# Low parts of 22 weight chunks in two attentions: GpSimd subtracts instead of VectorE

## The reference, cut to what matters

```python
qz = h @ w_in                                   # 1024 x 4096: q of 24 heads, z
q = rms_norm(q, q_norm_g) * (HEAD_DIM ** -0.5)
o, lse = dilated_group_attn(q[:, :, hs], kb, vb, slopes[hs], window, d)   # three groups
alpha = jax.nn.softmax(jnp.stack(lses), axis=0)
y = o.reshape(bsz, s, B_WIDTH) * jax.nn.silu(z)
```

```python
y_a = chunked_attention(q.reshape(shp), k.reshape(shp), v.reshape(shp), rel_table) @ w_attn_out
y_b = conv_module(c_in, conv_glu_bias, conv_dw_w, conv_dw_b, conv_ln_g, conv_ln_b, conv_w_out)
gates = jax.nn.sigmoid(g + gate_bias)
```

## Time and profile before

| what | us |
|---|---|
| median of 3 runs | 1925.88 (1925.7 to 1926.75) |
| profiled execution, span | 1924.0 |
| PE busy | 1830.6 (95%) |
| DVE busy | 1047.5 (54%) |
| ACT busy | 736.8 (38%) |
| POOL busy | 53.2 (3%) |
| low parts on DVE (L1827) | 149, 337.2 busy, mean 2263 ns |

### The profile page before, as it was taken

The page is one execution under the profiler, slowest core; times in us unless marked ns, Lnnn a source line. Parts: engine busy times, 40 slices in busy tenths (PEclk is TensorE's granted clock), DMA queues, the critical chain, the costliest instruction groups (busy, mean ns, idle before and its releaser), DMA issues.

```text
span 1924.0 us, 22231 instructions
## 1 busy us (share of the span) xinstructions
PE 1830.6 (95%) x8618; PEld 1492.9 (78%) x8618; DVE 1047.5 (54%) x1498; ACT 736.8 (38%) x1008; POOL 53.2 (3%) x103
## 2 busy tenths in 40 slices
PE   4999999989999999999999999998999999999998
PEld 3788888856877777778888887986666788888887
DVE  6336666458566666754444314699775463333213
ACT  4445554224355656432323214223462342323212
POOL 1000001000000000100000000000000000000000
PEclk8999999989999999999999999999999999999999
DMA  8346565422322221233342323232223223342321
GB/s 329 134 131 188 176 176 174 150 77 67 86 66 66 66 61 50 70 104 90 88 125 82 119 89 88 88 110 70 63 66 110 88 69 106 87 119 78 121 88 66
DMA packets 246679, 201.10 MB, mean 105 GB/s; under 512 B 6386, under 2 KB 225860, under 8 KB 245572
## 3 DMA queue, kind: packets, MB, share of 16 engines
q1 hardware_dynamic: 238048, 166.25, 29.3%
q0 software_dynamic: 8064, 33.56, 5.0%
q10 hardware_dynamic: 484, 0.16, 0.0%
HBM read 197.83 MB, written 2.11 MB: 104 GB/s over the span
## 4 chain that ended last, share of the span: by engine, by line
PE 77%; DVE 13%; ACT 5%; issue 3%; DMA 1%; DVEq 0%; SPq 0%; POOL 0%; ACTq 0%; POOLq 0%
PE acc L699 13%; PE acc L701 13%; PE acc L700 13%; PE sc L1064 6%; DVE s_s_row L2163 4%; PE acc L1064 3%; DVE s_w_low L1827 2%; PE tr L1064 2%; ACT s_w_high L1323 2%; PE ob L1064 2%; PE misc L1064 2%; DMA s_ada_w<-in_a_ada_w 1%; PE sc L699 1%; PE sc L701 1%; PE sc L700 1%
## 5 line engine op out<-in xcount | busy, mean ns | idle before, releaser
L1827 DVE TENSOR_TENSOR s_w_low<-s_raw,s_w_high 128x2048 fp32r<-128x2048 f32 (+1 forms) x149 | 337.2, 2263 | 356.4 <-ACT s_w_high L1323 356.4
L1323 ACT ACTIVATE s_w_high<-s_raw 128x2048 fp32r<-128x2048 f32 x151 | 284.6, 1885 | 205.0 <-PE acc L1064 174.6
L699 PE MATMUL acc<-s_h_high,s_w_high 128*128 128x512 f32 x880 | 345.1, 392 | 1.6 <-DVE s_sg L2399 1.6
L701 PE MATMUL acc<-s_h_high,s_w_low 128*128 128x512 f32 x880 | 342.5, 389 | 0.0
L700 PE MATMUL acc<-s_h_low,s_w_high 128*128 128x512 f32 x880 | 342.5, 389 | 0.0
L699 PEld LDWEIGHTS acc<-s_h_high,s_w_high 128*128 128x128 f32 x880 | 165.3, 188 | 37.2 <-issue 4.1
L701 PEld LDWEIGHTS acc<-s_h_high,s_w_low 128*128 128x128 f32 x880 | 165.2, 188 | 34.6
L700 PEld LDWEIGHTS acc<-s_h_low,s_w_high 128*128 128x128 f32 x880 | 165.3, 188 | 33.7 <-issue 0.2
L1699 ACT ACTIVATE s_hid_high<-s_hd 128x512 fp32r<-128x512 f32 x44 | 27.8, 632 | 219.3 <-DVE s_hd L2408 119.0
L890 PE MATMUL acc<-s_h_high,s_w_high 128*128 128x512 f32 x256 | 107.3, 419 | 2.2 <-DVE s_w_low L1827 1.4
L699 PE MATMUL acc<-s_b_high,s_w_high 128*128 128x512 f32 x224 | 91.7, 410 | 11.3 <-DVE s_b_low L1876 7.3
(11 more groups left out here) (446 smaller groups left out, 3353.7 us busy)
## 6 DMA issues: line engine op xcount, KB each, us to landing
s_raw<-in_a_w_in SPq DMA_DIRECT2D x48, 512.0 KB, 5.0
s_raw<-in_ffn_w_gate SPq DMA_DIRECT2D x44, 512.0 KB, 4.0
s_raw<-in_ffn_w_up SPq DMA_DIRECT2D x44, 512.0 KB, 5.2
s_raw<-in_ffn_w_down SPq DMA_DIRECT2D x40, 512.0 KB, 4.2
s_raw<-in_w_in SPq DMA_DIRECT2D x36, 512.0 KB, 4.4
s_raw<-in_b_w_in SPq DMA_DIRECT2D x32, 512.0 KB, 4.8
s_ada_w<-in_b_ada_w POOLq DMA_DIRECT2D x24, 512.0 KB, 4.9
s_ada_w<-in_a_ada_w POOLq DMA_DIRECT2D x8, 1024.0 KB, 12.6
```

What stands on the lines that cost most here:

```text
L699: pe.matmul(bank[b][:, :], w_high[:, o:o + P], hi, start=(k == 0), stop=False, skip_group_check=grouped)
L701: mm = pe.matmul(bank[b][:, :], w_low[:, o:o + P], hi, start=False, stop=(k == nk - 1), skip_group_check=grouped)
L1323: act.activation(w_high[:, part], raw[:, part], ACT.Copy).then_inc(w_high_ready, 1)
L1827: dve.tensor_tensor(w_low[:, w], raw[:, w], w_high[:, w].bitcast(F32), ALU.subtract).then_inc(w_ready, 1)
```

## The change

GpSimd gets a helper `low_part(c)`, which waits for the high part of chunk c, subtracts, and counts `w_ready` up. It does so for chunks 1 to 15 of "qz", for the two of "bo" as before, and for chunks 1 to 7 of "gates"; `tile_sum` moves between the third and the fourth of those. VectorE loses the same 15 subtractions in the loop over (s, n) and seven of the eight in the loop over rows; the one at n = 29, for the first chunk of the next phase, stays with it. All other orders stay.

```diff
--- before.py
+++ after.py
@@ -668,10 +668,16 @@
                                    pattern=[[-1, P]], channel_multiplier=1).then_inc(dist_ready, 1)
 
 
+            def low_part(c):
+
+                w = slice(c % 2 * SLOT, (c % 2 + 1) * SLOT)
+                pool.wait_ge(w_high_ready, c + 1)
+                pool.tensor_tensor(w_low[:, w], raw[:, w], w_high[:, w].bitcast(F32), ALU.subtract).then_inc(w_ready, 1)
+
+            for j in range(1, 16):
+                low_part(C0["qz"] + j)
             for s in range(2):
-                pool.wait_ge(w_high_ready, C0["bo"] + s + 1)
-                w = slice(s * SLOT, (s + 1) * SLOT)
-                pool.tensor_tensor(w_low[:, w], raw[:, w], w_high[:, w].bitcast(F32), ALU.subtract).then_inc(w_ready, 1)
+                low_part(C0["bo"] + s)
 
             def tile_sum():
 
@@ -682,7 +688,11 @@
                 pool.wait_ge(cy_added, 2)
                 pool.tensor_tensor(ln[0][:, :], ln[0][:, :], ln[1][:, :], ALU.add).then_inc(cy_added, 1)
 
-            tile_sum()
+            for g in range(1, 8):
+                if g == 4:
+                    tile_sum()
+                low_part(C0["gates"] + g)
+
         @block.tensor
         def _(pe):
             def product(b, tq, s, where, t, high, low, k0, nk, ready=None, base=0, between=None, bank=acc):
@@ -2235,7 +2245,6 @@
                 dve.reciprocal(tiny[:, Q_R + 12 * (s % 2):Q_R + 12 * (s % 2) + 12], tiny[:, Q_RT:Q_RT + 12])\
                    .then_inc(qr_ready, 1)
 
-            low = None
             a = NQ - 1
             for s in range(NQ):
                 for n in range(4):
@@ -2243,9 +2252,6 @@
                     before = (s - 1, n - 1) if n > 0 else (s - 2, 3)
                     if before[0] >= 0:
                         scale(*before)
-                    if low is not None:
-                        next_low(*low)
-                        low = None
                     if n == 3:
                         query_means(s)
                     if s > 1 and n == 1:
@@ -2260,8 +2266,6 @@
                         query_rstd(s)
                     if s > 1 and n == 2:
                         y_rest(s - 2)
-                    if t is not None and t % 2 == 0 and t < 4 * NQ - 2:
-                        low = q0 + t // 4, t // 2 % 2
             scale(a - 1, 3)
             tops(a, 0)
             near_row(a, 1)
@@ -2564,7 +2568,7 @@
                 e0 = EARLY[1] + 6 * PER_CHUNK + PER_ROW * n
                 for e in range(e0, min(e0 + PER_ROW, len(taps))):
                     tap(e)
-                if n % 4 == 1:
+                if n == H2 * TT - 3:
                     next_low(q0 + n // 8, n // 4 % 2)
                 conv_norm(n - LN_AT)
             scale2(H2 * TT - 1)
```

## The result

The changed kernel takes 1945.62 us in the median of 4 runs (1944.16 to 1946.35), the kernel before beside it 1926.32 (1925.7 to 1927.85): a ratio of 1.0097, 95% interval 1.0084 to 1.011, slower. Forecast were 1942 and a range of 1929 to 1953.

The account below looks back on a forecast made before the run. TensorE was taken as the bound, except VectorE in the second attention while it has convolution taps. First attention 5.1, port 8.2 and clock 3.4 sum to +16.7 on 1924.0, plus 1.9 to the median: 1942, range 1929 to 1953.

Parts of the forecast that it names:

- Start of the first attention: First attention's first chunks: low parts come late with little or no slack, costing 2.3 + 1.3 + 1.7 = 5.3 us.
- Steady slots: Five first-attention slots: 2.34 us gained and 2.6 lost in each, taken as +0.1 to +0.3 a slot, +0.5 in all.
- Last slot: First attention, 738 to 768 us: its single chunk is 0.3 us late, but its rows come sooner, -0.7.
- Port: Second attention: GpSimd's subtraction blocks VectorE operations that need both read paths, +8.2 us, bounds -1.5 and +10.0.
- the two ways: Second attention: GpSimd gets in between two taps, sum 10.0 us, or after them, 6.1; the middle was taken.
- chunk 7: Second attention: GpSimd works from 1426.4 to 1431.0 us and holds L2550; rows behind have no slack, 2.25 us.
- Chunk 6: Second attention: GpSimd works from 1409.3 to 1413.9 us and holds L2541; the row behind is 2.3 us later.
- Clock: Second attention: longer TensorE waits lower its clock, 1.7 us a stretch, two taken, +3.4 us, bounds 0 and +14.
- (b): Second attention: only scalings are stopped, taps and L2541/L2550 run on; +3.6 us in all, 1929.5; chance 0.15.
- (c): First attention: GpSimd's subtraction is not waited for, steady slots keep 2.34 us each; -8 or so, 1918; chance 0.06.
- (d): First attention: 2.0 us waits of the steady slots lower the clock too, +10 us on top, 1952; chance 0.13.

Follow-up runs that it names:

- the version that gains: Against the kernel before, GpSimd makes the first attention's 15 low parts in two halves, TensorE first waiting for the first half alone: 1908.84 us, ratio 0.9908.
- the one with added waits: Against the kernel moving only the second attention's seven subtractions, GpSimd also waits for the row's taps at chunks 1 to 3: 1930.69 us, ratio 1.0025.

## Why the prediction was right, and where it was not

- **Start of the first attention, 5.3.** Right: waits of 2.19 and 1.18 us for the first two chunks and 3.66 for the third; the first head's scores come 3.8 us later (3.6 forecast) and the next slot is 1.6 longer (1.7 forecast), 5.4 in all.
- **Steady slots, +0.5.** Right, step by step: 33.98 in place of 33.90 us, with 0.33 us of wait at n = 2 (0.6 forecast) and 1.79 at the next head's chunk (2.0 forecast, "2 us or more"). The gain was 2.55 us rather than 2.34, since a slot without waits is 31.35.
- **Last slot, -0.7.** -0.6.
- **Port, +8.2.** The mechanism was right: taps and L2545 are held, and of the two ways GpSimd took "in between taps". By row: 2.2, 2.1, 1.0, -0.8, 0, 2.2 for chunks 1 to 6 against 2.45, 2.45, 1.1, -0.6, 0, 2.3. The term that failed is chunk 7, 2.25 forecast and 0.3 measured. The step took the place of L2550 from the trace of before without removing the moved subtraction from ahead of it. Chunk 6 was priced by the same faulty step and came out right by luck. Without the subtraction VectorE is free at 1422.4, 0.8 us before GpSimd starts at 1423.17, and L2545 would have run ahead of it. It didn't only because it also waits for ScalarE's s_ln, which ScalarE makes behind the high part and which the prediction doesn't name (the changed kernel's ACT):

```profile
1422.97 0.72 ACT L1784 ACTIVATE s_ln<-s_cy,s_derived 128x512 f32<-128x512 f32 x1
```

The middle of the two ways hid the error: that branch's own sum was 10.0, and 6.9 was measured. (The middle of 6.1 and 10.0 is 8.05, not 8.2.) In the first attention one scaling a slot was to be held and cost nothing; in the steady slots none is.
- **Clock, +3.4.** Mis-sized: 4.6 us in the second attention, since three windows were lowered and not two, and 1.6 in the first attention. The rest of the 19.5 us, 1.2, lies outside both attentions, most of it behind the wait in 1540 to 1590 us, where the clock is 0.93 in place of 0.97 though the change touches nothing there.
- **Rivals.** (b) fell with the taps of 6.32 us. (c) fell with the waits at L900. (d) holds in part: waits of 1.8 us were followed by a lowered clock in one steady slot of the changed kernel and in two places of the kernel with that attention alone, not in each slot. The wait of 3.66 us at 554.91 in the changed kernel was followed by none (1.00 in 550 to 570), while the same wait of 3.65 us in the kernel with that attention alone was followed by 0.75 over 6.8 us. So the size of a wait alone doesn't tell where the clock falls. The argument against (d), that waits of up to 1.8 us left the clock at 1.00, had a counterexample in the trace of before, in the first attention's last slot, behind waits of 1.61 and 1.08 us:

```profile
765.00:770.00 5.00, 5.00 (x27) 4.29 (x26) 1.72 (x8) 4.78 (x8) 0.00 (x0) 0.73 0.01 2
```
- The forecast of 1942 is 3.6 us short of 1945.6. Of these 0.6 is rounding: 1924.0 + 16.7 + 1.9 is 1942.6. The other 3.0 are the port, 1.3 too many (8.2 against 6.9), the clock, 2.8 too few (3.4 against 6.2), 1.2 outside the attentions, and 0.3 in smaller terms and between trace and median. That the time fell so near is in part luck: errors of both signs cancel.

What I had not looked for is the version that gains: the time between a chunk's first and second tile was in the trace of before all along, 6.5 us for the chunk of n = 2 (616.63 to 623.15) and 9.1 for the next head's (597.82 to 606.93). Halves were tried in the first attention alone.

## What to carry to other kernels

Moving work to a slower, idle engine pays only where its result isn't awaited; if it is, ask which part of it the consumer reads first, and deliver and signal that part first (here, for the 15 chunks of the first attention, 0.45% slower became 0.9% faster with the same work on the same engine). The costs of two late results don't simply add up: what stays behind on the relieved engine can make the moved piece late as well. And when the place of an operation is read from the trace of before, first take out of it what the change removes, since that may be what put the operation there.

## What the hardware showed that was not expected

- A GpSimd instruction with two inputs gets in between VectorE's back-to-back taps: it took 4.90 us in place of 4.58, so by this reading waited about 0.3, while each tap lasts 0.7. From then on the next tap waited for all of it (6.32 us for the three in place of 2.07). A bias addition with one operand in PSUM and a maximum of one SBUF input ran beside it at their usual 0.29 us.
- GpSimd clearing memory holds a one-input scaling of VectorE (1.72 us in place of 0.29) but not taps with two inputs in SBUF (2.07).
- The clock had a mean of 0.77 to 0.82 in 15 us around waits of 5.64, 3.91 and 3.92 us, and of 0.83 in 10 us of one steady slot whose longest wait is 1.8. Behind a wait of 3.66 us it stayed at 1.00 in one kernel, and behind one of 3.65 us at the same place it was 0.75 over 6.8 us in another. It did not fall where 44 matmuls without a use filled the three waits; they saved 4.6 us. In code that no kernel here changes, around one and the same wait of 3.62 us (1540 to 1590 us), it was 0.93, 0.97 or 1.00 from one kernel's trace to the next, and from that wait to the end of the span the traces of the changed kernel, the kernel before and the one with added waits take 371.9, 370.9 and 369.5 us: 2 to 3 us of difference between two kernels may be no more than that.
- Two subtractions of 1024 columns on GpSimd take 2.4 us each, 4.74 together, against 4.58 for one of 2048: to split costs 0.16 us.
